# Moving the moving operands XH and XL by 64 bytes in SBUF

## What is computed

```
px = (rmsnorm(x, norm1_g[l]) * (1.0 + sc1) + sh1) @ w_in[l] + b_in[l]
x = x + g1 * (y_x @ w_out[l])
x = x + g2 * swiglu(rmsnorm(x, norm2_g[l]) * (1.0 + sc2) + sh2, w_gu[l], w_down[l])
h = x @ w_in          # second block, mixers a and b
gate = sigmoid(x @ ple_w_gate[i])
```

## The kernel before

| buffers | first byte | modulo 128 | modulo 256 |
|---|---|---|---|
| `raw`/`w_lo` (4), `w_hi` (2) | 16,512 to 36,992, every 4,096 | 0 | 128 |
| `X` | 57,600 | 0 | 0 |
| `XH`, `XL` | 82,176 and 106,752 | 0 | 0 |
| `XH2`, `XL2`, `X2` (views on the bytes of XH and XL) | 98,560, 114,944, 82,176 | 0 | 0 |
| `tri` and all that follows | from 131,328 | | |
| `wgh`, `wgl` | 146,496 and 147,008; 64 bytes for each k | 64, then 0, in turn | |
| `HH`, `HL` | 149,184 and 173,760 | 64 | 192 |
| `YH2`, `YL2` | 143,808 and 160,192 | 64 | 192 |
| `PH`, `PL`, `PWH`, `PWL` | 208,320, 212,416, 198,080, 189,888 | 64 | 192 |

## Time and profile before

### The profile page before, as it was taken

One profiled execution on the slowest core, in us unless ns is written; L12 is line 12 of the kernel. 1 busy time (PEld: TensorE's weight loads), 2 busy tenths in 40 slices (PEclk: granted clock), 3 DMA queues, 4 the chain that ended last, 5 costly groups with the idle time before them and its releaser, 6 DMA issues.

```text
span 2586.4 us, 39643 instructions
## 1 busy us (share of the span) xinstructions
PE 2522.5 (98%) x14594; PEld 2083.7 (81%) x14594; DVE 1386.4 (54%) x2065; ACT 776.3 (30%) x1620; POOL 1544.1 (60%) x1625
## 2 busy tenths in 40 slices
PE   6999999999999999999999999999999999999999
PEld 4888988888888886888788887778888888777876
DVE  5864556742853758726433333444444545556754
ACT  3224353111111123244321212222222222443544
POOL 3433245765766665543777777776666676556563
PEclk9999999999999999999999999999999999999999
DMA  7341142332333322121233232433333333323231
GB/s 280 107 155 41 34 179 86 127 130 65 122 130 98 119 60 69 58 66 42 83 96 94 93 98 82 130 106 100 91 103 96 93 103 94 98 73 98 83 106 65
DMA packets 79264, 255.57 MB, mean 99 GB/s; under 512 B 9872, under 2 KB 13712, under 8 KB 78864
## 3 DMA queue, kind: packets, MB, share of 16 engines
q1 hardware_dynamic: 63136, 213.21, 25.8%
q10 hardware_dynamic: 15984, 40.40, 5.1%
HBM read 236.28 MB, written 2.10 MB: 92 GB/s over the span
## 4 chain that ended last, share of the span: by engine, by line
PE 88%; DVE 4%; issue 3%; POOL 2%; ACT 2%; DMA 1%; SPq 0%; ACTq 0%; POOLq 0%; DVEq 0%
PE PS L463 21%; PE PS L466 21%; PE PS L464 21%; PE PS L1668 4%; PE PS L1670 4%; PE PS L1669 4%; PE PS L725 1%; POOL w_lo L444 1%; PE PS L714 1%; PE PS L708 1%; DMA raw<-in_wout 1%; PE PS L1524 1%; POOL w_hi L442 1%; DVE Z L2425 1%; DVE XL L2432 1%
## 5 line engine op out<-in xcount | busy, mean ns | idle before, releaser
L444 POOL TENSOR_TENSOR w_lo<-raw,w_hi 128x512 fp32r<-128x512 f32 (+1 forms) x606 | 880.5, 1453 | 50.6
L463 PE MATMUL PS<-XH,w_hi 128*128 128x512 f32 (+1 forms) x2080 | 782.7, 376 | 16.5 <-DVE XL L2432 3.3
L464 PE MATMUL PS<-XL,w_hi 128*128 128x512 f32 (+1 forms) x2080 | 755.6, 372 | 0.0
L466 PE MATMUL PS<-XH,w_lo 128*128 128x512 f32 (+1 forms) x2080 | 707.2, 373 | 0.0
L437 POOL TENSOR_TENSOR word<-ones 128x1 f32<-128x1 f32 x303 | 93.7, 309 | 869.4 <-PE PS L466 544.2
L463 PEld LDWEIGHTS PS<-XH,w_hi 128*128 128x128 f32 x2080 | 392.2, 189 | 118.6 <-issue 9.3
L442 POOL TENSOR_SCALAR w_hi<-raw 128x512 fp32r<-128x512 f32 (+1 forms) x606 | 482.0, 795 | 0.0
L464 PEld LDWEIGHTS PS<-XL,w_hi 128*128 128x128 f32 x2080 | 392.4, 189 | 70.0
L466 PEld LDWEIGHTS PS<-XH,w_lo 128*128 128x128 f32 x2080 | 362.5, 188 | 55.1
L1668 PE MATMUL PS<-XH,w_hi 128*128 128x512 f32 (+1 forms) x640 | 230.9, 361 | 8.4 <-DVE XL L2432 8.4
L1670 PE MATMUL PS<-XH,w_lo 128*128 128x512 f32 (+1 forms) x640 | 224.9, 351 | 0.0
(11 more groups left out here) (346 smaller groups left out, 3507.0 us busy)
## 6 DMA issues: line engine op xcount, KB each, us to landing
raw<-in_wgu SPq DMA_DIRECT2D x88, 512.0 KB, 3.5
raw<-in_wa SPq DMA_DIRECT2D x80, 512.0 KB, 3.5
modt<-in_wmod SPq DMA_DIRECT2D x48, 512.0 KB, 9.9
raw<-in_win SPq DMA_DIRECT2D x48, 512.0 KB, 3.5
modv<-in_wmod ACTq DMA_DIRECT2D x48, 512.0 KB, 4.7
raw<-in_wdn SPq DMA_DIRECT2D x32, 512.0 KB, 3.6
QS<-Z ACTq DMA_DIRECT2D x96, 128.0 KB, 2.6
raw<-in_wout SPq DMA_DIRECT2D x16, 512.0 KB, 3.5
```

Source lines behind the costliest of these rows:

```text
L444: pool.tensor_tensor(lo, src, hi.bitcast(FP32), ALU.subtract).then_inc(s_split, 1)
L463: pe.matmul(acc(s)[:, a:b], hi, rh[:, i, a:b], start=i == 0, stop=False)
L464: pe.matmul(acc(s)[:, a:b], hi, rl[:, i, a:b], start=False, stop=False)
L466: last = pe.matmul(acc(s)[:, a:b], lo, rh[:, i, a:b], start=False, stop=i == k - 1)
```

## The change

Two buffers of 64 bytes that nothing uses are placed, one ahead of XH and one behind XL. XH, XL and their views (XH2, XL2, X2, XF, the six modulation tiles) start 64 bytes later, at 64 modulo 128. What follows XL moves by 128 bytes and keeps its residue modulo 128; modulo 256 it goes to the other half (HH, HL, YH2, YL2 from 192 to 64). The weights lie ahead of both and stay. No instruction is added, removed or moved.

```
         X = place("X", [P, KT, T])
+        place("lead", [P, 16])
         XH = place("XH", [P, KT, T], FP32R)
         XL = place("XL", [P, KT, T], FP32R)

+        place("lead2", [P, 16])
         tri = place("tri", [P, 2, P])
```

## The result

The changed kernel takes 2591.36 us (median of 11 runs, 2589.82 to 2594.12); the kernel before, run beside it, 2585.69 (2583.15 to 2588.71). The ratio is 1.0021, with a 95% interval of 1.0012 to 1.0029: some 5.7 us (3 to 7.5) slower. The forecast was 2564.0, faster, with a range up to 2587; the measured time lies above it.

The account below looks back on a forecast made before the run. TensorE's split matmuls were taken to bound the kernel. XH's gains, 13.7 + 5.6 + 4.2 + 0.9 = 24.4 us, times 0.93 gave 22.6, so 2586.6 - 22.6 = 2564.0 us; range 2559 to 2587.

Parts of the forecast that it names:

- What bounds the kernel: Whole kernel: TensorE's matmuls busy 98% of the span, six split-product lines 76.0% of the chain, POOL's splitting not ahead.
- 22.6 forecast for XH at HH's rate: XH's split-product steps: 24.4 us priced, times 0.93 for the share on the chain, gives 22.6 us gained; chance 0.66.
- 24.4 us priced: Sum over XH's matmul steps and tile parts, 13.7 + 5.6 + 4.2 + 0.9, before the share on the chain.
- The rates of before: Start-to-start k-steps before the change: XH 0.697 to 0.700 us against HH's 0.687 at 512 columns; 1.049 to 1.060 against 1.039 at 768.
- 13.7 and 4.2 us: XH at 512 columns: gains of 11 ns each for 1248 line-463 steps and 384 tile parts between mLSTM steps.
- the 5.6: XH's 416 steps of 768 columns: 128 x 21 ns + 288 x 10 ns, a 5.6 us gain.
- the 0.9: 256 tile parts of 256 columns between the mLSTM steps: 3.5 ns each, a 0.9 us gain.
- The slower rival: XH, HH, YH2 steps: distance to weights counts modulo 256, only 64 ahead fast; about 7 us lost, 2593.6; chance 0.08.
- The embedding's products: Weights and moving operand both high, both at 64: 0.226 then 0.231 us each, so neither residue nor place explains both.
- Place: Rival: XH's low neighbourhood in SBUF or another buffer property, not its residue, costs; no change, 2586.6; chance 0.18.
- Half the gain: Rival: XH at 64 gets only to the gates' halfway rate, 1.044 a step; 11.3 us gained, 2575.3; chance 0.08.
- What lies on the same bytes: ScalarE's writes into XH2, DVE's operands, XF's weights, opening loads and output stores at the new residue: costed at nothing.

## Why the prediction was wrong

- *What bounds the kernel: right.* TensorE's rate sets the time. Steps that became 10 ns shorter by XH's address alone gave 17.6 us (2586.02 to 2568.46; 14.5 to 21.5 by the interval); steps that became longer cost 7.8 (what follows XL moved alone). The 22.6 forecast for XH at HH's rate was too much: of the 24.4 us priced 72% arrived (59 to 88), not 93%, and where the rest stayed is not shown.
- *The rates of before: right.* XH was slow against HH by its address, and bringing it to HH's distance, 64 modulo 256, brought it to HH's rate (0.687 and 1.040).
- *The step that failed* is "By the addresses HH, HL, YH2 and YL2 start at 64 modulo 128, XH, XL and the weights at 0", with what follows from it, that after the change "the split products have one kind of residue, the faster one". They did come to one kind, but the residue counts modulo 256 and from the weights: 64 ahead is fast, 64 behind (192) is not, and modulo 128 the two look alike. So none of the gains priced for XH at 512 columns (13.7 and 4.2 us) came; the steps went from between 0.697 and 0.700 up to 0.700. At 768 columns 128 x 13 ns + 288 x 2 ns = 2.2 us came for the 5.6, and at 256 columns 256 x 16 ns = 4 us for the 0.9, if all parts run as the timeline's seven steps do. With XH alone moved the kernel's time stayed within -0.10 to 0.08%.
- *What was priced at nothing* was the move of what lies behind XL. The two pads together move HH and YH2 by 128 bytes, which modulo 128 is no move. 176 x 13 + 176 x 8 + 216 x 13 ns = 6.5 us is what their steps lost, against 7.8 measured for that move alone (4.4 to 10.1).
- *The slower rival was the right one*, with 0.08: it named the distance modulo 256, HH and YH2 as the place, and 2593.6 against the measured 2591.36. Its sign that HH's step goes above 0.69 while XH's stays near 0.697 is what the trace shows. It had no gain of XH at 768 columns (1.060 to 1.047), and its condition that only 64 ahead is fast does not hold: distance 0, which the change does not produce, is faster still at 512 columns (0.681).
- *The embedding's products* were read as equal residues modulo 128. Modulo 256, too, PH and PL start where PWH and PWL do, at distance 0, and they keep it under every move tried. The 0.226 of the first stretch is that distance's pace (0.681/3 = 0.227), the 0.231 of the later one is not, and in the changed kernel the first stretch takes 2.52/11 = 0.229:

```profile
2253.12 0.40 PE L839 MATMUL PS<-PH,PWH 128*128 128x512 f32 x1
...
2255.64 0.39 PE L841 MATMUL PS<-PH,PWL 128*128 128x512 f32 x1
```

So something besides the distance also sets a pace, and what it is stays open.

- *Place* fell with the weights alone moved. *Half the gain* fell with XH alone moved.
- *What lies on the same bytes: right.* ScalarE's copies and the output's stores stayed:

```profile
L1007 ACT ACTIVATE YH<-ZS x8: 632/632/634, 1759.9 to 2214.3; 128x512 fp32r<-128x512 f32 x8
L1007 ACT ACTIVATE XH<-ZS x8: 629/632/635, 2375.0 to 2478.2; 128x512 fp32r<-128x512 f32 x8
```

```profile
out_dram<-X SPq DMA_DIRECT2D x8, 256.0 KB, 3.0
```

- The Trainium skill's page "SBUF — State Buffer", section "Who interferes with whom", has the two read ports of TensorE independent and TensorE waiting on nobody. As far as speed goes this case's runs do not agree with a pace that leaves the two operands independent: the weights alone, moved by 64 bytes, changed the step of an unmoved XH from 0.697 to 0.686 us. Where the time goes no run shows.

## What to carry to other kernels

When two residues explain a difference in rate, write down the addresses of both operands at every modulus that separates the cases, and ask which of them the change will actually produce: here the fast and the new case agree modulo 128 and differ modulo 256, and the trace of before held no example of the new one. A pad moves everything behind it, so the buffers that run well are to be checked as closely as the ones that are to be helped. Where matmuls follow one another without a gap, two small variants (pad the moving operand, pad the weights) show whether addresses matter, and start-to-start distances show it more clearly than the total.

## What was not expected of the hardware

In these split products, fp32r matmuls with a weight load for each, the pace goes with the distance modulo 256 between moving and stationary operand: from 0.681 us for three of 512 columns at distance 0 to 0.702 at 160, 3%. It does so in nearly all stretches read, but one of XH at distance 64 took 0.700, and the embedding's products, at distance 0 throughout, took 0.226 to 0.231 a matmul. The best distance depends on the shapes: 0 is the fastest at 512 columns alone and among the slowest where 512 and 256 alternate (1.053 against 1.040 at 64). Multiples of 32 that are not multiples of 64 were slow in all four cases tried (0.700 to 0.702). Why a distance is fast was not settled: for HH, with `w_hi` and `w_lo` at different distances the step was slower than at either.
